# The reciprocal square root of eleven norms: Sqrt on ScalarE and a reciprocal on VectorE, instead of Ln and Exp on ScalarE

## The reference, cut to what matters

```python
def rms_norm(x, g):
    xf = x.astype(jnp.float32)
    y = xf * lax.rsqrt(jnp.mean(xf * xf, axis=-1, keepdims=True) + EPS)
    return (y * g.astype(jnp.float32)).astype(x.dtype)
...
        x = x + rms_norm(m, p['post_mix_g'][layer])
        h = rms_norm(x, p['pre_ffn_g'][layer])
        f, cs = conv_ffn(h, conv_prev[layer], p['w_up'][layer], p['conv_w'][layer],
                         p['conv_b'][layer], p['w_down'][layer])
        x = x + rms_norm(f, p['post_ffn_g'][layer])
```

## Time and profile before

| | before |
|---|---|
| median of 3 runs | 1741.18 us (1739.67 to 1741.36) |
| span of the profiled execution, first to last instruction | 1737.2 us |
| TensorE busy, matmul and weight load | 91%, 83% |
| VectorE, ScalarE, GpSimd busy | 57%, 37%, 13% |
| mean granted TensorE clock | 0.951 of 2.4 GHz |
| table loads on ScalarE | 27, of 1283 ns each |

### The profile page before, as it was taken

The page is one execution under the profiler, slowest core; times in us unless marked ns, Lnnn a source line. Parts: engine busy times, 40 slices in busy tenths (PEclk is TensorE's granted clock), DMA queues, the critical chain, the costliest instruction groups (busy, mean ns, idle before and its releaser), DMA issues.

```text
span 1737.2 us, 32432 instructions
## 1 busy us (share of the span) xinstructions
PE 1584.2 (91%) x11908; PEld 1441.5 (83%) x11908; DVE 989.3 (57%) x1652; ACT 644.5 (37%) x1038; POOL 225.6 (13%) x388
## 2 busy tenths in 40 slices
PE   4897999977999999995997999899995999999997
PEld 3797998977999999995984666544594999999996
DVE  3343664247888884336545656415636888886333
ACT  3444443234222223335515555423435222223333
POOL 0000000002322221002002111000002223322000
PEclk9898999999999999998997999897998999999998
DMA  6132222321232322332213434210021333332331
GB/s 195 51 95 61 74 72 66 94 73 49 86 96 88 93 80 84 90 102 97 74 35 96 115 107 108 79 33 7 1 77 33 89 93 90 91 93 68 97 92 57
DMA packets 250794, 138.16 MB, mean 80 GB/s; under 512 B 28412, under 2 KB 246578, under 8 KB 250696
## 3 DMA queue, kind: packets, MB, share of 16 engines
q1 hardware_dynamic: 242080, 126.20, 25.2%
q0 software_dynamic: 4256, 8.89, 1.6%
q10 hardware_dynamic: 4376, 2.00, 0.5%
HBM read 133.74 MB, written 3.67 MB: 79 GB/s over the span
## 4 chain that ended last, share of the span: by engine, by line
PE 83%; DVE 7%; ACT 4%; issue 2%; ACTq 0%; DVEq 0%
PE psum L574 65%; PE psum L915 3%; PE psum L901 2%; DVE x L1505 2%; PE psum L937 2%; PE psum L1002 2%; PE psum L1028 2%; DVE ut L1502 1%; PE psum L1027 1%; PE psum L1045 1%; PE psum L694 1%; PE psum L1037 1%; DVE xl L1490 1%; ACT wh L1090 1%; ACT lat_h L1359 1%
## 5 line engine op out<-in xcount | busy, mean ns | idle before, releaser
L574 PE MATMUL psum<-xh,wh 128*128 128x260 f32 x2112 | 436.0, 288 | 48.8 <-DVE xl L1490 33.6
L1469 DVE TENSOR_TENSOR wl<-ws,wh 128x1024 fp32r<-128x1024 f32 x221 | 270.7, 1226 | 366.4 <-ACT wh L1090 364.4
L574 PE MATMUL psum<-xh,wl 128*128 128x260 f32 x2112 | 431.1, 286 | 0.0
L574 PE MATMUL psum<-xl,wh 128*128 128x260 f32 x2112 | 431.0, 286 | 0.0
L1090 ACT ACTIVATE wh<-ws 128x1024 fp32r<-128x1024 f32 x221 | 233.3, 1056 | 527.7 <-PE psum L574 527.7
L574 PEld LDWEIGHTS psum<-xh,wh 128*128 128x128 f32 x2112 | 332.4, 193 | 53.8 <-issue 33.5
L574 PEld LDWEIGHTS psum<-xh,wl 128*128 128x128 f32 x2112 | 331.5, 192 | 0.0
L574 PEld LDWEIGHTS psum<-xl,wh 128*128 128x128 f32 x2112 | 331.4, 192 | 0.0
L574 PE MATMUL psum<-acth,wh 128*128 128x260 f32 x704 | 142.4, 283 | 0.0
L574 PE MATMUL psum<-acth,wl 128*128 128x260 f32 x704 | 141.6, 282 | 0.0
L574 PE MATMUL psum<-actl,wh 128*128 128x260 f32 x704 | 141.3, 282 | 0.0
(11 more groups left out here) (248 smaller groups left out, 2312.0 us busy)
## 6 DMA issues: line engine op xcount, KB each, us to landing
ws<-in_w_up SPq DMA_DIRECT2D x88, 512.0 KB, 3.8
ws<-in_w_in_a SPq DMA_DIRECT2D x32, 512.0 KB, 4.0
ws<-in_w_down SPq DMA_DIRECT2D x32, 384.0 KB, 3.4
cn<-in_cache_ckv SPq DMA_DIRECT2D x96, 128.0 KB, 2.0
ws<-in_w_down SPq DMA_DIRECT2D x32, 320.0 KB, 3.1
ws<-in_w_out_a SPq DMA_DIRECT2D x16, 512.0 KB, 4.0
cn<-in_cache_ckv POOLq DMA_DIRECT2D x32, 128.0 KB, 2.4
ws<-in_w_o SPq DMA_DIRECT2D x8, 512.0 KB, 4.5
```

The lines of the kernel that those rows point to most:

```text
L574: mm = pe.matmul(psum[:, 2 * slot + b, 0:HB], w, r[:, k, b * HB:(b + 1) * HB], start=st, stop=en)
L1469: dve.tensor_tensor(wl[:, slot2, :], ws[:, slot4, :], f32(wh[:, slot2, :]), ALU.subtract).then_inc(w_low, 1)
```

## The change

ScalarE's part ends with one activation, Sqrt, whose result is the standard deviation and not its reciprocal. The semaphore `ln_done` becomes `sd_done`. A new helper `rms` on VectorE waits for it, takes the reciprocal of the 520 columns in place, signals `r_ready`, and waits for that itself. It stands where VectorE used to wait for `r_ready`, at each of the eleven norms. TensorE's waits on `ln_done` are now on `sd_done`; its wait on `r_ready` for v stays and is now answered by VectorE.

```diff
-            def rms(name, dst):
+            def deviation(name, dst):
                 g = GI[name]
 
-                act.activation(warm[:, :], ones[:, 0:1], ACT.Ln)
+                act.activation(warm[:, :], ones[:, 0:1], ACT.Sqrt)
                 act.wait_ge(ss_done, g + 1)
-                act.activation(halves(dst[:, :]), psum[:, 6:8, 0:HB], ACT.Ln, bias=eps[:, 0:1], scale=1.0 / GROUPS_SQ[g][2]).then_inc(ln_done, 1)
-                act.wait_ge(ln_done, g + 1)
-                act.activation(dst[:, :], dst[:, :], ACT.Exp, scale=-0.5).then_inc(r_ready, 1)
+                act.activation(halves(dst[:, :]), psum[:, 6:8, 0:HB], ACT.Sqrt, bias=eps[:, 0:1], scale=1.0 / GROUPS_SQ[g][2]).then_inc(sd_done, 1)
...
+            def rms(name, dst):
+
+                dve.wait_ge(sd_done, GI[name] + 1)
+                dve.reciprocal(dst[:, :], dst[:, :]).then_inc(r_ready, 1)
+                dve.wait_ge(r_ready, GI[name] + 1)
+
...
             def update(p, m):
 
-                dve.wait_ge(r_ready, GI[["", "m_sgu", "m_ffn0", "m_attn", "m_ffn1"][p]] + 1)
+                rms(["", "m_sgu", "m_ffn0", "m_attn", "m_ffn1"][p], r2)
...
                 if first:
-                    dve.wait_ge(r_ready, 1)
+                    rms("x0", r1)
...
                 if first:
-                    dve.wait_ge(r_ready, GI["v"] + 1)
+                    rms("v", r2)
...
                     if first:
-                        dve.wait_ge(r_ready, GI["x1" if l == 0 else "x3"] + 1)
+                        rms("x1" if l == 0 else "x3", r1)
...
-            dve.wait_ge(r_ready, GI["x2"] + 1)
+            rms("x2", r1)
...
-            dve.wait_ge(r_ready, GI["kv"] + 1)
+            rms("kv", r2)
...
             rotate(krt[:, :], krr[:, :], psum[:, 4:6, 0:HB], ut[:, 0, :], rotk_done, rotk_step, 0)
-            dve.wait_ge(r_ready, GI["cq"] + 1)
+            rms("cq", r2)
```

More of the change, by code:

```diff
@@ L278, in trunk @@
         w_high, w_low, mm_done = S("w_high"), S("w_low"), S("mm_done")
-        sq_done, sq_added, ss_done, ln_done, r_ready = S("sq_done"), S("sq_added"), S("ss_done"), S("ln_done"), S("r_ready")
+        sq_done, sq_added, sq_summed, ss_done, sd_done, r_ready = (S(n) for n in (
+            "sq_done", "sq_added", "sq_summed", "ss_done", "sd_done", "r_ready"))
         x_new, u_mul, xh_ready, xl_ready, xkh_ready, xkl_ready = (S(n) for n in (
@@ L607, in rms @@
                 before = sqa[:, :] if n > 2 else sq[:, 0, :]
-                wait(pe, ln_done, g)
+                wait(pe, sd_done, g)
                 for b in range(2):
@@ L654, in _ @@
             pe.wait_ge(d_gate, 16)
-            pe.wait_ge(ln_done, 1)
+            pe.wait_ge(sd_done, 1)
             for g in range(GROUPS):
@@ L707, in _ @@
             pe.wait_ge(mix_read, KG)
-            pe.wait_ge(ln_done, GI["v"] + 1)
+            pe.wait_ge(sd_done, GI["v"] + 1)
             for g in range(4):
@@ L838, in _ @@
             pe.wait_ge(rotk_step, 2)
-            pe.wait_ge(ln_done, GI["cq"] + 1)
+            pe.wait_ge(sd_done, GI["cq"] + 1)
             for h in range(H):
@@ L1176, in _ @@
                 if u == 0:
-                    rms("x0", r1)
+                    deviation("x0", r1)
                 value_tile(0, u)
@@ L1192, in gate_tile @@
                     ahead(U_U, 4, i, u)
-                    rms("v", r2)
+                    deviation("v", r2)
                     act.wait_ge(rT_done, 1)
@@ L1235, in _ @@
             wo(3)
-            rms("m_sgu", r2)
+            deviation("m_sgu", r2)
             update(1)
@@ L1247, in tile @@
                     if first:
-                        rms("x1" if l == 0 else "x3", r1)
+                        deviation("x1" if l == 0 else "x3", r1)
                     q, j = 4 * i + u, 2 * i + u // 2
@@ L1287, in mlp @@
                     down(3, e, guard=True)
-                rms(g, r2)
+                deviation(g, r2)
             mlp(0)
@@ L1294, in _ @@
             ahead_static(U_KV)
-            rms("x2", r1)
+            deviation("x2", r1)
             for t in range(KC):
@@ L1304, in _ @@
             ahead_static(U_DQ)
-            rms("kv", r2)
+            deviation("kv", r2)
             for t in range(KQ):
@@ L1313, in _ @@
             act.wait_ge(ckt_ready, KC)
-            rms("cq", r2)
+            deviation("cq", r2)
             for j in range(4):
@@ L1453, in _ @@
             ahead_static(U_O + KD - 1)
-            rms("m_attn", r2)
+            deviation("m_attn", r2)
             update(3)
```

## The result

| | before | after |
|---|---|---|
| median | 1740.43 us (1739.19 to 1741.36, 4 runs) | 1758.84 us (1756.12 to 1761.24, 4 runs) |
| ratio, 95% interval | | 1.0104 (1.0089 to 1.0119) |
| span of the profiled execution | 1737.2 us | 1759.6 us |
| VectorE, ScalarE busy | 989 us, 644 us | 1026 us, 618 us |

The change makes the kernel slower, by 18.4 us in these runs. The forecast was 1764 us, within 1752 to 1781. The changed kernel was timed once more later (the experiment "The changed kernel again"): 1752.65 us against 1740.83, a ratio of 1.0076 (1.0061 to 1.0092). So the loss is 12 to 18 us.

The account below looks back on a forecast made before the run. TensorE, busy 91% of the span, was taken as the bound. Norms +18.7, kv +1.3, cq +1.5 and the attention's load +1.3 made +22.8 us: span 1737.2 to 1760.0, plus 4.0 outside, 1764.0 us; range 1752 to 1781.

Parts of the forecast that it names:

- What stands on the path: TensorE waits fully for nine norms (x0, v, m_sgu, x1, m_ffn0, x2, m_attn, x3, m_ffn1): together +18.7 us.
- R - 1.92: Cost in us per fully exposed norm: reciprocal's time plus 0.06 of hand-overs, minus 1.98 for removed load, Exp and gaps.
- The size of R: Duration of VectorE's 520-column reciprocal in each norm: 4.0 us, bounds 3.4 to 5.5.
- the one-column rows on 8 partitions: VectorE profile rows: reciprocal 151 ns against 142 and 146, giving 6.3 to 10.3 ns per column; 128 partitions showed 153 against 153.
- kv: At this norm Sqrt starts some 0.8 us earlier, but the reciprocal still stops TensorE: +1.3 us.
- cq: At this norm, hidden before, the reciprocal delays the first evacuation and TensorE stops: +1.5 us.
- The load before the attention's Exp: ScalarE must load Exp's table before the samples' first Exp, since Sqrt's is now loaded: +1.3 us, once.
- Square and Copy without loads of their own: Rival on ScalarE: Sqrt's table set lacks them, so 11 more loads, 14 us more, 1778; chance 0.03.
- The clock: TensorE's slow 1.2 GHz stretches behind x0, x1, x2, x3 and partly v are already paid: nothing added.
- A further fall at cq: Rival: TensorE's clock falls once more at kv or cq, 2.9 to 5.8 us more, 1767 to 1770; chance 0.12.
- The rival of the column rate: VectorE's reciprocal runs like an ordinary pass, 0.69 us, and the kernel is faster, 1731.4 us; chance 0.16.
- The 4.0 us around the span: Time outside the profiled span, by which the median 1741.2 exceeded 1737.2; taken as untouched by the change.

Follow-up runs that it names:

- the one column: The changed kernel with the reciprocal taken of one column only, the other 519 left out; 1725.26 us against 1741.88 for the kernel before, ratio 0.9890.
- 7.0 us of reciprocals: The changed kernel with two more reciprocals of 260 columns in each norm; 1800.78 us, ratio 1.0330 to the kernel before.

## Why the prediction was right, point by point

- **What stands on the path** was right. Nine norms fully, each by 1.49 us where R - 1.92 gives 1.48 with the measured R. The doses bear the formula out: with the one column 16.6 us gained (sum 15.8), with 7.0 us of reciprocals 58.9 lost (sum 54; the surplus is of the size of the 5.6 us that TensorE was busy longer).
- **The size of R** is the term that was mis-sized: "Between 6.3 and 10.3 I take 7.4 ns" a column, 4.0 us; measured 6.25 ns and 3.40 us. The lower end of 3.4 us was exact, and in part by luck: it added a difference of 5 ns between two different operations to 1.3 ns a column, in which the fixed part of 0.15 us was contained already. The sign came from the one-column rows on 8 partitions, and the choice of that pair was luck as well. That the 8-partition rows have the shorter fixed part may be so (520 columns take 3391 ns there and 3402 on 128 partitions), but 11 ns in the fixed part give no reason why one pair should show the cost of a column and the other not. The pair on 128 partitions misled, most likely because two operations differ in their fixed part by as much as one column costs; no run measured that of the multiplication. By the Trainium skill (VectorE: DVE Perf Modes, the walkthrough of the eight slices), with its repeat count of 8 read as 8 cycles a column, the estimate was 4.3 us; the measurement decides, and is 0.9 us lower.
- **With R = 3.40** the nine norms give 13.3 us, kv 0.65, cq 0.93. kv measured 0.57. cq measured 0.52 in one execution and nothing in the other; my count of its tiles at 0.12 us a matmul left out some 0.3 us at their start. Together 14.4 to 14.9, against 18.4 and 11.8 measured.
- **The load before the attention's Exp** (+1.3 us) was wrong. I took the load to stand behind the wait; it stands ahead of it and fits into ScalarE's idle time.
- **12 table loads in place of 27, and Square and Copy without loads of their own**: as forecast. This rival fell.
- **The clock**: that the falls behind x0, x1, x2 and x3 were already paid holds within 1 us; TensorE was busy for 812.8 and 811.4 us in the first stretch, where it was 811.7 before, and for 448 us in the last, as before. A further fall at cq came in one of two executions, and where it came it hid the stop that I had counted.
- **The rival of the column rate** needed 0.69 us for the reciprocal and fell with the first row.
- **The 4.0 us around the span** were wrong: two profiled executions whose own time is known lie 1.6 and 1.7 us above their span (1761.24 and 1759.6, 1752.32 and 1750.6). So the execution profiled before was a quick one. The forecast was made against the median, and did not suffer.

Two errors, R too large by 0.6 us (6.6 us in the sum) and the load of 1.3 us, point the same way. The first runs came out 4 us above the sum with the measured R, and that made up for half of the errors; in the one that was profiled the slower attention did it. That the forecast of 1764 us lies as close as 5 us to the first median is therefore partly luck. From the second, 1752.65 us, it is 11 us away, and that median lies at the very end of the range. The mechanism and the sign hold in both.

## What to carry to other kernels

The reciprocal of fp32 on VectorE costs 6.25 ns a column on 8 partitions as on 128. For 520 columns that is eight times a multiplication of the same tile by a constant (431 ns). A row that is the same on all partitions pays it in full, and it should be moved off the path or kept to a few columns. Before trading table loads for another engine's work, look for one activation that yields the whole function: it removed load, second activation and hand-over together. A price can be had before the first run from one-column instructions only if their fixed parts are known; a second width tells it at once.

## What the runs showed that I had not expected

- A table load is issued ahead of the semaphore wait of its activation at the Exp of the samples, so it hides in idle time there (959.73, then 0.25 us idle). At the first Gelu of layer 0 it is not: there it starts at 55.50, behind 4.31 us in which ScalarE stood idle until VectorE's first value tile was there (54.73 + 0.70).
- Two executions of one program differ by 10 us in a stretch that the change does not touch, with granted clocks of 0.88 and 0.85.
- Shorter stops gave back more than their own length: 25 us where 17 or 18 were removed. The granted clock was 1.00 behind stops of 1.6 us (x0) and 1.5 us (x2), where it had been 0.50 and 0.61 behind 3.6 and 3.5 us. In the one-column kernel it was 0.72 from 52 to 58, behind a stop of 1.8 us at x0, and 1.00 behind one of 1.7 us at x2. What decides between the two stays open.
